# Inverses of the triangular blocks from compact 32-row diagonal blocks, with products in four row tiles

## The reference, cut to what matters

```python
def wkv7_step(S, inp):
    r, w, k, v, a, b = inp
    sa = jnp.einsum('bhvk,bhk->bhv', S, a)
    S = S * w[:, :, None, :] + sa[..., None] * b[:, :, None, :] + v[..., None] * k[:, :, None, :]
    return S, jnp.einsum('bhvk,bhk->bhv', S, r)
...
    for d in range(2):
        S0 = jnp.zeros((B, RW_HEADS, RW_N, RW_N), jnp.float32)
        S_c, yc_d = direction(cx, d, S0)
        _, yl_d = direction(lat, d, S_c)
```

```python
    hid = jax.nn.silu(jnp.einsum('becd,edf->becf', xs, w1)) * jnp.einsum('becd,edf->becf', xs, w3)
    ys = jnp.einsum('becf,efd->becd', hid, w2) * gate[..., None].astype(h.dtype)
```

## Time and profile before

| what | us |
|---|---|
| median of 3 runs | 3021.54 (3018.71 to 3033.44) |
| the profiled execution | 3028.37, of which its span in the trace 3026.6 |
| `rwkv_prepare`, context / latent | 2235.0 to 2296.2 / 2378 to 2437 |
| `rwkv_inverse`, context / latent | 2296.2 to 2357.1 / 2436.8 to 2496.8 |
| `rwkv_chunks`, context / latent | 2357 to 2378 / 2497 to 2527 |
| `experts` with the output | 2527 to 3026.6 |

### The profile page before, as it was taken

How to read it: one execution, slowest core, us unless ns; L and a number is a source line. 1 busy time by engine, 2 the same in 40 slices (tenths; PEclk the granted TensorE clock), 3 DMA queues, 4 the chain that set the end, 5 groups by cost and what they waited for, 6 DMA issues and landing times. The chain is left out here.

```text
span 3026.6 us, 44774 instructions
## 1 busy us (share of the span) xinstructions
PE 2654.6 (88%) x19672; PEld 1646.5 (54%) x19672; DVE 1331.0 (44%) x2509; ACT 490.1 (16%) x1158; POOL 26.4 (1%) x48
## 2 busy tenths in 40 slices
PE   7989999999988999998999989879969798866655
PEld 3457844446767888735753333345438697433323
DVE  2775488442473876586321111131366763100001
ACT  1023200000213000225221111020051311200000
POOL 0000000000000000000000000000000000000000
PEclk9999999999999999998999999989989899978888
DMA  9530255342342676220169999972110007899998
GB/s 357 195 139 22 91 195 222 141 165 111 112 195 70 250 278 247 74 84 29 59 237 403 428 427 428 428 317 51 41 38 29 2 4 317 362 426 428 427 426 354
DMA packets 67938, 651.34 MB, mean 215 GB/s; under 512 B 14880, under 2 KB 26912, under 8 KB 28064
## 3 DMA queue, kind: packets, MB, share of 16 engines
q1 hardware_dynamic: 67744, 648.47, 53.1%
HBM read 644.12 MB, written 4.33 MB: 214 GB/s over the span
## 5 line engine op out<-in xcount | busy, mean ns | idle before, releaser
L375 PE MATMUL ps<-HT,ring 128*128 128x256 f32 (+1 forms) x3152 | 909.7, 447 | 13.2 <-ACT HT L669 4.9
L375 PEld LDWEIGHTS ps<-HT,ring 128*128 128x128 f32 x3152 | 594.1, 191 | 294.0 <-issue 235.5
L2438 PE MATMUL ps<-ring,arena 128*32 128x256 f32 (+1 forms) x2944 | 368.2, 501 | 112.0 <-DMA ring<-in_moe_w 102.7
L477 DVE SCALAR_TENSOR_TENSOR acc<-ring,sil,acc 128x512 f32<-128x512 f32 x616 | 411.7, 745 | 0.0
L375 PE MATMUL ps<-arena,ring 128*128 128x256 f32 (+3 forms) x1232 | 373.0, 463 | 3.4 <-PEq L718 2.2
L2438 PEld LDWEIGHTS ps<-ring,arena 128*32 128x32 f32 (+1 forms) x2944 | 139.6, 129 | 317.7 <-issue 195.1
L375 PEld LDWEIGHTS ps<-arena,ring 128*128 128x128 f32 (+2 forms) x1232 | 229.9, 188 | 138.9 <-issue 118.8
L1037 DVE SCALAR_TENSOR_TENSOR XT<-ps,modcols,XT 128x256 f32<-128x256 f32 x124 | 55.8, 481 | 277.9 <-PE ps L375 140.4
L2459 PE MATMUL ps<-ring,conv 128*64 128x512 f32 x496 | 112.3, 596 | 24.4 <-DMA ring<-in_moe_w 23.7
L2459 PE MATMUL ps<-ring,arena 128*32 128x256 f32 x960 | 79.6, 488 | 61.6 <-DMA ring<-in_moe_w 61.6
L495 ACT ACTIVATE modrows<-ps 128x128 f32<-128x128 f32 x44 | 12.2, 277 | 574.8 <-PE ps L491 574.8
(11 more groups left out here) (431 smaller groups left out, 2576.3 us busy)
## 6 DMA issues: line engine op xcount, KB each, us to landing
ring<-in_moe_w SPq DMA_DIRECT2D x184, 2048.0 KB, 25.6
ring<-in_w_mod SPq DMA_DIRECT2D x24, 2048.0 KB, 8.2
ring<-in_ada_w SPq DMA_DIRECT2D x24, 2048.0 KB, 8.1
ring<-in_w_up SPq DMA_DIRECT2D x16, 2048.0 KB, 12.3
ring<-in_w_down SPq DMA_DIRECT2D x16, 2048.0 KB, 12.4
ring<-in_w_in SPq DMA_DIRECT2D x10, 2048.0 KB, 10.3
ring<-in_od_w_in SPq DMA_DIRECT2D x6, 2048.0 KB, 25.5
arena<-in_moe_w SPq DMA_DIRECT2D x10, 1024.0 KB, 20.5
```

The costliest lines, as they stand in the source:

```text
L375: last = nc.tensor.matmul(bank_of(job, j), lhsT, rhs, start=n == 0, stop=n == len(terms) - 1)
L477: ins = nc.vector.scalar_tensor_tensor(out=acc, in0=weights[:, k, :], scalar=s, in1=acc, op0=ALU.mult, op1=ALU.add)
L2438: last = nc.tensor.matmul(K.ps[M * j:M * j + M, 2 * (e % 2) + i, 0:FW], xs[:, e // 4 % 2, e % 4, 4 * h + k, :], weights((m, e, h), k, slic ...
```

## The change

`rwkv_inverse` no longer works on full 64x64 blocks. Each 64x64 triangular matrix is split in two 32x32 diagonal blocks (`b` = 0 and 1) and one 32x32 corner. The diagonal blocks of both heads stand under each other: partitions 0 to 31 and 32 to 63 for the even head, 64 to 95 and 96 to 127 for the odd one (`quarter(e, b)`), and 16 of them side by side make 512 columns. So X, XT, Z and N's transpose need 512 columns instead of 1024 each, and a whole direction fits in one PSUM bank. Doubling runs over levels 1 to 4 within the diagonal blocks. The last doubling is one job pair for both directions: `corner_z`, then the corner of the inverse.

- Jobs: 26 instead of 56. Each is 64 matmuls of 32x32 on 32 columns, in the order row tile 0, 1, 2, 3, instead of 16 of 64x64 on 64 columns.
- `rwkv_prepare`: a direction's "n" groups (4 groups of 16 matmuls) become "x" and "nT" (2 groups of 64 matmuls). One group "corner" of 64 matmuls is added, evacuated by ACT.
- DVE in `rwkv_inverse`: 26 evacuations of 128x512 instead of 56, 4 instructions of the start instead of 12. The start of direction 1's XT goes to POOL (two 128x512 operations), which also clears a new buffer `solver` for each direction before it clears `uv`.
- ACT copies the diagonal blocks of XT into `solver` (8 copies of 32x16x32, and 2 for the corner of direction 1, DVE making 2 for that of direction 0), and `rwkv_chunks` reads `solver` at the solve.
- Constants: six levels of 64 columns become five of 32, with a new mask `strict`.

```diff
 def product_groups(s):
...
-        groups += [("n", d, half, t) for half in range(2) for t in range(2)]
+        groups += [("x", d, 0, 0), ("nT", d, 0, 0)] + [("corner", d, 0, 0)] * d
...
-                    lhs, rhs = ((w.ar, w.bk), (w.bk, w.ar))[h]
-                    for i in range(8 * part, 8 * part + 8):
-                        for rows in (slice(0, 64), slice(64, 128)):
-                            last = nc.tensor.matmul(K.ps[rows, bank, i % 8 * CH:(i % 8 + 1) * CH], lhs[rows, i, 0, :], rhs[rows, i, 0, :],
-                                                    start=True, stop=True)
+                    lhs, rhs = (w.ar, w.bk) if kind == "x" else (w.bk, w.ar)
+                    for i in range(16):
+                        for e in range(2):
+                            for b in range(2):
+                                rows, t = slice(64 * e, 64 * e + 64), slice(HALF * b, HALF * b + HALF)
+                                last = nc.tensor.matmul(K.ps[quarter(e, b), bank, i * HALF:(i + 1) * HALF], lhs[rows, i, 0, t], rhs[rows, i, 0, t],
+                                                        start=True, stop=True)
...
 def rwkv_inverse(K, m, also=()):
...
-    nc, levels = K.nc, 6
-    parts = [(d, half) for d in range(2) for half in range(2)]
+    nc, levels = K.nc, 5
     jobs = []
     for i in range(1, levels):
-        jobs += [(i, "z", d, q) for d, q in parts]
-        jobs += [(i, kind, d, q) for d, q in parts for kind in (("x", "xT") if i < levels - 1 else ("xT",))]
+        jobs += [(i, "z", 0), (i, "z", 1), (i, "x", 0), (i, "xT", 0), (i, "x", 1), (i, "xT", 1)]
+    jobs += [(levels, "z", 0), (levels, "xT", 0)]
...
-                for c in range(8 * q, 8 * q + 8):
-                    for rows in (slice(0, 64), slice(64, 128)):
-                        last = nc.tensor.matmul(K.ps[rows, j % NBANK, c % 8 * CH:(c % 8 + 1) * CH], lhs[rows, c, :], rhs[rows, c, :],
-                                                start=True, stop=True)
+                for c in range(16):
+                    out = K.ps[:, j % NBANK, c * HALF:(c + 1) * HALF]
+                    for e in range(2):
+                        for b in range(2):
+                            if i == levels:
+                                side = m.of[b]
+                                lhs, rhs, at, to = ((m.corner, side.x, quarter(e, b), quarter(e, 1 - b)) if kind == "z" else
+                                                    (m.corner_z, side.xT, quarter(e, 1 - b), quarter(e, b)))
+                            else:
+                                lhs, rhs = {"z": (w.nT, w.x), "x": (w.xT, w.z), "xT": (w.z, w.xT)}[kind]
+                                at = to = quarter(e, b)
+                            last = nc.tensor.matmul(out[to], lhs[at, c, :], rhs[at, c, :], start=True, stop=True)
                 last.then_inc(*K.inc("inverse_product"))
...
         @block.gpsimd
         def _(pool):
+            begin(nc.gpsimd, 1, "masked").then_inc(*K.inc("transposed"))
+            for w in m.of:
+                K.step(pool, nc.gpsimd.memset(w.solver, 0.0), "cleared")
```

More of the change, by code:

```diff
@@ L42 @@
 CH = 64
+HALF = CH // 2
 GRID_W = 64
@@ L2720, in rwkv_buffers @@
     m.reset = ring[:, 13312:14336]
+    m.corner, m.corner_z = (buf[:, 13824:14336].rearrange("p (i c) -> p i c", i=16) for buf in (ring, A))
     m.bonus = four(ring, 14336)
@@ L2795, in rwkv_prepare @@
     per_bank = 512 // used
-    on_act = [kind in ("tok", "v") for kind, _, _, _ in groups]
+    on_act = [kind in ("tok", "v", "corner") for kind, _, _, _ in groups]
     def kept(g):
@@ L2907, in _ @@
                 ps = K.ps[:, g % NBANK, :]
-                if kind == "tok":
+                if kind == "corner":
+                    last = nc.scalar.activation(m.corner, by_tile(g % NBANK, HALF), ACT.Copy)
+                elif kind == "tok":
                     last = nc.scalar.activation(m.of[d].tok[:, 4 * part:4 * part + 4].rearrange("p i c -> p (i c)"), ps, ACT.Copy)
@@ L3005, in _ @@
         def _(dve):
-            for d, q in parts:
-                x = half(m.of[d].x[:, 0], q)
-                nc.vector.tensor_tensor(x, x, eye, ALU.add).then_inc(*K.inc("inverse_begun"))
-            for d, q in parts:
+            for w in m.of:
+                nc.vector.tensor_tensor(w.x, w.x, eye, ALU.add).then_inc(*K.inc("inverse_begun"))
+            begin(nc.vector, 0, "transpose_blocks").then_inc(*K.inc("transpose_begun"))
+            for j, (i, kind, d) in enumerate(jobs):
                 w = m.of[d]
-                x = half(w.x[:, 1], q)
-                K.step(dve, nc.vector.tensor_tensor(x, half(w.n[:, 1], q), level(1 - d, 0), ALU.mult), "transpose_blocks")
-                nc.vector.tensor_tensor(x, x, eye, ALU.add).then_inc(*K.inc("transpose_begun"))
@@ L3014, in _ @@
-            for j, (i, kind, d, q) in enumerate(jobs):
-                w = m.of[d]
-                ps = K.ps[:, j % NBANK, :].rearrange("p (i c) -> p i c", c=CH)
-                dve.wait_ge(*K.at("inverse_product", j + 1))
-                if kind == "z":
-                    last = nc.vector.tensor_tensor(half(w.n[:, 0], q), ps, level(d, i), ALU.mult)
-                else:
-                    if kind == "x":
-                        dve.wait_ge(*K.at("inverse_product", where[i, "xT", d, q] + 1))
-                    x = half(w.x[:, 0 if kind == "x" else 1], q)
-                    last = nc.vector.tensor_tensor(x, x, ps, ALU.add)
+                ps = K.ps[:, j % NBANK, :].rearrange("p (i c) -> p i c", c=HALF)
@@ new lines, in _ @@
+                dve.wait_ge(*K.at("inverse_product", j + 1))
+                if i == levels and kind == "z":
+                    last = nc.vector.tensor_copy(m.corner_z, ps)
+                elif i == levels:
+                    dve.wait_ge(*K.at("cleared", 2))
+                    for e in range(2):
+                        last = nc.vector.tensor_copy(w.solver[quarter(e, 0), :, HALF:CH], ps[quarter(e, 0)])
+                elif kind == "z":
+                    last = nc.vector.tensor_tensor(w.z, ps, spread(m.level[:, d, i, :]), ALU.mult)
+                else:
+                    a = w.x if kind == "x" else w.xT
+                    last = nc.vector.tensor_tensor(a, a, ps, ALU.add)
@@ L3025, in _ @@
                 last.then_inc(*K.inc("inverse_kept"))
+        @block.scalar
+        def _(act):
+            act.wait_ge(*K.at("cleared", 2))
+            for d, w in enumerate(m.of):
+                act.wait_ge(*kept(levels - 1, "xT", d))
+                for e in range(2):
+                    for b in range(2):
+                        nc.scalar.activation(w.solver[quarter(e, b), :, HALF * b:HALF * b + HALF], w.xT[quarter(e, b)], ACT.Copy)
+            act.wait_ge(*K.at("inverse_product", len(jobs)))
+            ps = K.ps[:, (len(jobs) - 1) % NBANK, :].rearrange("p (i c) -> p i c", c=HALF)
+            for e in range(2):
+                nc.scalar.activation(m.of[1].solver[quarter(e, 1), :, 0:HALF], ps[quarter(e, 1)], ACT.Copy)
@@ L3115, in solve @@
                     rows, i = slice(64 * h, 64 * h + 64), 4 * b + c
-                    last = nc.tensor.matmul(K.ps[0:64, solution(d, h), b * CH:(b + 1) * CH], w.x[rows, 1, i, :],
+                    last = nc.tensor.matmul(K.ps[0:64, solution(d, h), b * CH:(b + 1) * CH], w.solver[rows, i, :],
                                             m.rhs[rows, d, b, :], start=True, stop=True)
@@ L3265, in constant_tables @@
     out["causal"][:] = np.tile(np.concatenate(causal, 1), (2, 1))
-    for i in range(6):
+    s, u = np.arange(HALF)[:, None], np.arange(HALF)[None]
+    for i in range(5):
         b = 1 << i
```

74 lines of the change are left out of this document (47 added, 27 removed).

## The result

| | before | changed |
|---|---|---|
| median, us | 3024.65 (3018.71 to 3033.44, 4 runs) | 3125.06 (3121.57 to 3125.99, 4 runs) |
| ratio, 95% interval | | 1.0333 (1.0316 to 1.0349) |
| profiled execution, us | 3028.37 | 3124.91 |
| instructions in the profile | 44774 | 52314 |

The change makes the kernel slower by 3.3%. The forecast was 3105.0 us, with a range of 3065 to 3139.

A forecast was written before the change was run, and what follows sets the result against it. The prediction took PE's instruction supply to pace the inverses, about 3.8 us per 256 instructions. Inverses +75.5, prepare +4 and chunks +4 made +83.5 us on a median of 3021.5: 3105.0 us, range 3065 to 3139.

The forecast's parts named there:

- What bounds the stage: Both inverses: PE is paced by instruction supply, one packet of 256 instructions at a time; +37.3 and +38.2 us.
- Interval: Inverses: packets come 3.8 us apart (3.4 to 4.1), 25 after the first edge, for 98.2 us a stage.
- Work inside the packet interval: Inverses: each job is one packet, and its array time (0.93 us), DVE time and semaphore latency lie inside the interval.
- Starting operations on POOL: Start of the inverse: POOL's two 128x512 operations, needed by job 5, cost nothing, at most 2 us a stage.
- Prepare: Both prepare stages: 3 more instruction packets each, +3 us for context and +1 for latent, together +4 (-4 to +12).
- Chunks: Both chunks stages: the clock may begin at 0.50, about 2 us a stage, +4 us (0 to +15).
- Rival 1: Inverses: the array is the limit, not supply; 32 us a stage against 60, total 2962 us; chance 0.07.
- The floor per record: Inverses: no pair goes under 29.1 ns, evenly spread loads, +40 us a stage, total 3109 us; chance 0.08.

The follow-up runs named there:

- a_half_wide: Changed kernel with half the matmuls in both inverses, each with 64 columns in place of 32, streamed columns and evacuations kept: 3033.77 us.
- a_traffic: Changed kernel with 32 unused DMA transfers of 0.52 MB added in each inverse, two at a time: 3147.17 us.
- a_quarter_wide: Changed kernel with a quarter of the matmuls in both inverses, each with 128 columns, streamed columns and evacuations kept: 2985.64 us.
- a_prep_half: Changed kernel with half the matmuls for prepare's 32x32 products, each streaming 64 columns so that columns and evacuations stay: 3105.76 us.
- a_w_first: Changed kernel with prepare's large products (w, the transposes) ahead of the 32x32 ones in each direction, same instructions: 3128.79 us.
- a_warm: Changed kernel with four unused 128x512 matmuls added ahead of the products in each prepare: 3126.9 us.
- b_narrow: Kernel before with 32 of the 64 columns of each product streamed in both inverses, same instructions, loads and evacuations: 3098.05 us.
- b_diag: Kernel before with 8 matmuls on block diagonal 128x128 tiles per z job in place of 16 on 64x64: 3066.38 us, ratio 1.0133.
- b_waits: Kernel before with two waits on an already reached value added behind each matmul of the inverse: 3170.68 us.
- a_dve_begin: Changed kernel with the backward direction's first transpose in the inverse made on DVE in place of POOL: 3119.43 us.

## Why the prediction was right, and where it was off

**What bounds the stage.** Right. The runs of 127 to 128 pairs, the 26 packets, DVE's 3.2 us waits, the inverses of 100.0 and 102.9 us in a forecast of 90 to 105: each sign named ahead is there. a_half_wide (fewer instructions) and a_traffic (slower packets) show the cause from two sides. The sentence of the Trainium skill ("Runtime: NRT & Kernel Launch", Instruction fetch mechanics) that crossing a block is mostly hidden does not hold here, by 89.8 us of PE's idle time in 50 places.

**Interval.** The term was 25 x 3.8 + 3.2 = 98.2, short by 1.8 and 4.7 us a stage; +82.0 in place of +75.5. The 3.8 was right: in the middle of the stages 21 intervals take 78.1 us (2315.73 to 2393.84) and 80.0 us (2497.29 to 2577.30), 3.72 and 3.81 us each. The rows of before gave 3.4 to 3.99 and none decided between them, so that hit is in part luck. The missing time lies at the ends. In the context stage the last 115 pairs (from 2401.33) with the copies take 3.6 us in place of 1.9. In the latent one the last two full intervals are 4.9 and 4.7 us, where PE also waits 1.0 us for DVE in each.

**Work inside the packet interval.** Right: with a quarter of the instructions, but the same columns, DVE work and semaphores, the stage is 32 us (a_quarter_wide), and in the changed kernel the busiest engine works 51 of 100.

**Starting operations on POOL.** I took nothing, at most 2 us. It cost DVE 2.2 us (1.79 + 1.75 against 2 x 0.69) and made the first product come 1.1 us later (2306.71 - 2304.86 = 1.85 us into the stage against 0.74), but by the third packet nothing of that is left. A mechanism was missing, that POOL slows DVE while both run; the size holds.

**Prepare.** This is the step that failed in size: +4 (-4 to +12) against +17.2. The term counted packets and let the rest of PE's work stand at the prices of the earlier trace rows. But w and the transposes stand in those rows at a clock of 1.00, and in the changed kernel both directions run them at 0.50, at double the cost. That, 9.2 us, is the part left out; I had priced it for the chunks and not here. For the backward direction the runs show why: with the stops of 2.29 and 2.54 us ahead of it the clock is 0.50, without them (a_prep_half) it is 1.00. For the forward direction they don't: w is at 0.50 with a stop ahead of it (changed kernel), without one (a_prep_half), in first place (a_w_first) and behind extra work (a_warm). What they show is that in the context stage the 64x64 products ahead of it were followed by 1.00 and the 32x32 ones are not. The packets themselves were about right: 203 pairs, 406 instructions, ran before the first stop, where some 450 were expected to be at hand.

**Chunks.** +4.2 for a forecast of +4, and by the mechanism named: at 2404.90 the clock is at 0.50, and 1.00 only 4.7 us later.

```profile
2404.90:2409.60 4.70, 4.70 (x85) 4.58 (x87) 0.00 (x0) 0.77 (x2) 0.00 (x0) 0.50 0.01 3
2409.60:2427.90 18.30, 15.39 (x433) 13.62 (x429) 12.04 (x32) 2.32 (x7) 0.04 (x1) 1.00 0.01 3
```

**Rivals.** Rival 1 (no limit by supply) falls with a_half_wide; its 32 us are near the 31.8 and 33.4 of a_quarter_wide, which has a quarter of its loads. The floor per record falls with the 14 ns of a pair in these runs (128 in 1.80 us), even at the low clock.

**Open.** Why the forward w of prepare stays at a clock of 0.50. Why a packet takes 3.3 to 4.1 us with idle DMA engines, and why the latent stage with the same program took 100.0 to 103.1 us in different executions. Why b_narrow's clock stays down while PE is busy is not settled either: the run shows that it does, in both inverses, with half the columns.

## What to carry to other kernels

Count instructions beside columns. An f32 matmul here is four (two loads, two products; a transpose is only two, 16 pairs for 16 of them), so in a long run at 3.9 us for 256 a matmul costs about 60 ns; the 64x64 products of before, 58 ns of array time for two pairs, sat exactly there, and halving the tile doubled the count for work that was no longer the limit. Look for short idle times marked "issue" at every 126th pair: they say that an edge is near before any change is made.

When a change puts holes into PE's work or makes its products smaller, price the work behind them at the low clock as well, and take no duration from a row without its granted clock.

## What the runs showed of the hardware that I had not expected

- Half the streamed columns, with as many loads and matmuls and PE busy for 96.0 of 98.5 us, kept the granted clock at 0.50 and made the stage 38 us longer (b_narrow). 13.7 us of PE work without a gap left it at 0.50 too (a_prep_half).
- A weight load of 128 columns and its matmul of 64 take 114 ns at a granted clock of 1.00, four times the 29 ns at which pairs of 64x64 tiles follow each other (b_diag).
- A satisfied wait between matmuls costs: two in a row made each matmul 82 ns longer (b_waits).
- A masked multiplication on POOL stretched an addition on DVE from 0.69 to 1.79 us (changed kernel against a_dve_begin).
- DMA traffic of 235 GB/s that PE doesn't wait for moved the instruction packets from 3.6 to 4.7 us apart (a_traffic).
